# Moving the loop of spare blocks behind the static blocks in a mixture of experts, on one Trainium2 core

## The reference

```python
g_sel = argmax(softmax(h @ w_rg + b_rg))                  # 1 of 4 groups
e_p, e_idx = top_k(softmax(expert logits of that group), 2)  # 2 of its 8 experts
weights = g_p * e_p / sum(e_p)
# assignments sorted by expert, each expert's rows padded to blocks of 128
y = (silu(xb @ w_gate[e]) * (xb @ w_up[e])) @ w_down[e]   # one block of rows
out[token] += y * weight
```

## Time and profile before

| | us |
|---|---|
| median of 3 runs | 3689.51 (3687.7 to 3690.94) |
| the profiled execution | 3681.5 |
| its span, first to last instruction | 3679.7 |
| PE busy | 3420.4 (93%) |
| DVE busy | 1617.9 (44%) |
| ACT busy | 818.3 (22%) |
| POOL busy | 364.8 (10%) |

### The profile page before, as it was taken

How to read it: one execution, slowest core, us unless ns; L and a number is a source line. 1 busy time by engine, 2 the same in 40 slices (tenths; PEclk the granted TensorE clock), 3 DMA queues, 4 the chain that set the end, 5 groups by cost and what they waited for, 6 DMA issues and landing times. The chain is left out here.

```text
span 3679.7 us, 51768 instructions
## 1 busy us (share of the span) xinstructions
PE 3420.4 (93%) x20970; PEld 1738.1 (47%) x20970; DVE 1617.9 (44%) x2560; ACT 818.3 (22%) x1822; POOL 364.8 (10%) x355
## 2 busy tenths in 40 slices
PE   9999999899999899999998998998899978997996
PEld 4444665433333344777754333333455658553332
DVE  4750886510111475777756111113341875462114
ACT  0000650100000122555511000000233551111112
POOL 0010300210000000000000200000000820003110
PEclk9999999899999999999999999999999999999998
DMA  9990211599999621000023999997421402219996
GB/s 373 361 336 0 93 70 69 227 416 427 423 424 424 251 91 57 26 1 1 1 92 142 403 425 425 426 421 303 149 82 68 149 18 79 101 66 371 419 418 267
DMA packets 146694, 818.42 MB, mean 222 GB/s; under 512 B 29875, under 2 KB 35635, under 8 KB 100374
## 3 DMA queue, kind: packets, MB, share of 16 engines
q1 hardware_dynamic: 117910, 737.21, 50.1%
q0 software_dynamic: 25808, 68.88, 4.9%
q10 hardware_dynamic: 2736, 8.95, 0.6%
HBM read 752.52 MB, written 82.55 MB: 227 GB/s over the span
## 5 line engine op out<-in xcount | busy, mean ns | idle before, releaser
L2320 PE MATMUL m_yp<-m_w,m_hidT 128*32 128x512 f32 (+2 forms) x2248 | 378.9, 596 | 10.5 <-issue 4.6
L2297 PE MATMUL m_up<-m_w,m_xT 128*32 128x512 f32 (+2 forms) x1792 | 305.4, 608 | 20.3 <-DMA m_w<-in_moe_w_up 20.3
L2297 PE MATMUL m_gp<-m_w,m_xT 128*32 128x512 f32 (+2 forms) x1792 | 300.7, 598 | 9.8 <-DMA m_w<-in_moe_w_gate 5.4
L2078 DVE TENSOR_TENSOR m_hid<-m_sg,m_up 128x512 f32<-128x512 f32 x42 | 28.9, 688 | 573.9 <-PE m_up L2297 573.9
L2073 DVE TENSOR_TENSOR m_yt<-m_yp,keep_flat 128x512 f32<-128x512 f32 x128 | 82.5, 686 | 398.7 <-PE m_yp L2320 388.9
L2320 PEld LDWEIGHTS m_yp<-m_w,m_hidT 128*32 128x32 f32 (+2 forms) x2248 | 121.7, 124 | 219.6 <-issue 214.1
L2378 ACT ACTIVATE m_sg<-m_gp 128x512 f32<-128x512 f32 (+1 forms) x64 | 33.5, 524 | 786.1 <-PE m_gp L2297 539.2
L2297 PEld LDWEIGHTS m_up<-m_w,m_xT 128*32 128x32 f32 (+2 forms) x1792 | 104.2, 126 | 216.0 <-issue 216.0
L2297 PEld LDWEIGHTS m_gp<-m_w,m_xT 128*32 128x32 f32 (+2 forms) x1792 | 97.5, 124 | 206.7 <-issue 204.1
L434 PE MATMUL front_acc<-front_hT,front_wt 128*128 128x512 f32 x448 | 194.4, 594 | 0.4 <-DVE q0T L535 0.4
L1233 PE MATMUL n_acc<-n_wt,n_hT 128*128 128x512 f32 (+2 forms) x512 | 190.5, 528 | 2.0 <-DMA n_wt<-in_w_in 1.3
(11 more groups left out here) (505 smaller groups left out, 5032.8 us busy)
## 6 DMA issues: line engine op xcount, KB each, us to landing
m_w<-in_moe_w_gate SPq DMA_DIRECT2D x64, 2048.0 KB
m_w<-in_moe_w_up SPq DMA_DIRECT2D x64, 2048.0 KB
m_w<-in_moe_w_down SPq DMA_DIRECT2D x64, 2048.0 KB
v<-in_ada_w SPq DMA_DIRECT2D x40, 1024.0 KB
m_w<-in_moe_w_gate SPq DMA_DIRECT2D x32, 1024.0 KB
m_w<-in_moe_w_up SPq DMA_DIRECT2D x32, 1024.0 KB
m_w<-in_moe_w_down SPq DMA_DIRECT2D x32, 1024.0 KB, 30.2
v<-in_w_mod SPq DMA_DIRECT2D x24, 1024.0 KB
```

The lines of the kernel that those rows point to most:

```text
L2297: last = pe.matmul(acc[part, 0:F], xT[:, j, k, part], w[:, place_of[m_, r][0], k * F:(k + 1) * F], start=k == 0, stop=k == KC - 1)
L2320: last = pe.matmul(yp[e][part, :], hidT[:, k, part], w[:, place_of["d", r][0], k * D + e * 512:k * D + (e + 1) * 512], start=k == 0, stop= ...
```

## The change

Every engine's loop of spare blocks moves behind its static blocks. On SP all loads of the static blocks are issued without a stop, and the loads of the next stage's rows also come ahead of the loop; `AHEAD` goes, and a spare block now uses slots 0 to 2. On POOL the gather of block `DEEP` comes ahead of the spread and that of block `DEEP + 1` right behind it; the read of the table and its four operations become `sort_spills`, called in the loop over the static blocks at n = 3. Waits inside the loops' bodies are added, so that a spare block starts only when the static blocks are through; no body runs with these inputs. The computation of the static blocks is the same.

```diff
-    AHEAD = 2 * RING // 3
-    taken = {slot for _, _, slot, _ in layout.units[:AHEAD]}
-    spare = [s for s in range(RING) if s not in taken][:3]
+    spare = range(3)
...
                 place_rows()                       # DVE
-                for e in range(2):
-                    dve.sem_inc(so_y[e], 1)
-                spills = spilled(dve)
-                with dve.Fori(0, TURNS) as turn_no:
...
-                held(dve, st.marks, so_st, spills * (16 * GROUP) + 16)
                 copy_x(dve, dve.tensor_copy, 0, 0)
...
                 for e in range(2):
                     weigh_y(N - 1, e)
+                for e in range(2):
+                    dve.sem_inc(so_y[e], 1)
+                spills = spilled(dve)
+                with dve.Fori(0, TURNS) as turn_no:
...
-                for unit in layout.units[:AHEAD]:  # SP
+                for unit in layout.units:
                     load(*unit)
+                sp.wait_ge(d, at["gates"])
+                sp.wait_ge(sorted_out, 4)
+                for dst, row in ahead:
+                    sp.dma_start(dst, row).then_inc(ahead_in, 16)
+                sp.wait_ge(ahead_in, 16 * len(ahead))
                 spills = spilled(sp)
                 with sp.Fori(0, TURNS) as turn_no:
...
                 held(sp, st.marks, so_st, spills * (16 * GROUP) + 16)
-                for unit in layout.units[AHEAD:]:
-                    load(*unit)
...
+                def sort_spills():                 # POOL
+                    pool.wait_ge(t_st, 16 * 2 * T)
...
                 for n in range(DEEP):
                     gather(n)
+                gather(DEEP)
                 pool.wait_ge(filled, 16)
                 pool.wait_ge(d, at["places"])
                 for k in range(2):
                     for t in range(T):
                         pool.indirect_dma_start(out=row_table, ...).then_inc(t_st, 16)
-                pool.wait_ge(t_st, 16 * 2 * T)
...
+                gather(DEEP + 1)
+                for n in range(1, N):
+                    if n == 3:
+                        sort_spills()
+                    if n + DEEP + 1 < N:
+                        gather(n + DEEP + 1)
+                    scatter(n - 1)
+                scatter(N - 1)
                 spills = spilled(pool)
                 with pool.Fori(0, TURNS) as turn_no:
...
-                for n in range(DEEP, DEEP + 2):
-                    gather(n)
-                for n in range(1, N):
...
                 list_rows()                        # PE
+                keep_clock(pe, turn[0], ident, 4)
+                turn_x(0)
...
+                turn_hid(N - 1)
+                down(N - 1)
                 pe.sem_inc(so_dn, 1)
                 spills = spilled(pe)
                 with pe.Fori(0, TURNS) as turn_no:
...
                 act.sem_inc(so_st, 16)             # ACT
+                copy_x(act, act_copy, 0, 1)
...
+                copy_hid(N - 1)
                 spills = spilled(act)
                 with act.Fori(0, TURNS) as turn_no:
```

More of the change, by code:

```diff
@@ L2112, in _ @@
                     weigh_y(N - 1, e)
+                for e in range(2):
+                    dve.sem_inc(so_y[e], 1)
+                spills = spilled(dve)
+                with dve.Fori(0, TURNS) as turn_no:
+                    with dve.If(turn_no < spills):
+                        for j in range(GROUP):
+                            i = turn_no * GROUP + j
+                            dve.wait_ge(so_t, i + 1)
+                            dve.tensor_copy(xT[:, 0, half[0]], turn[0][:, :].rearrange("p (c s) -> p c s", c=4)).then_inc(so_cp[0], 1)
+                            dve.wait_ge(so_sg, i + 1)
+                            dve.tensor_tensor(hid[:, 0], sg[:, 0], up[0][:, 0:F], ALU.mult).then_inc(so_hid, 1)
+                            dve.wait_ge(stored[0], 16 * ((N + 1) // 2))
+                            dve.wait_ge(so_st, i * 16 + 16)
+                            dve.wait_ge(so_dn, i + 2)
+                            for e in range(2):
+                                dve.tensor_tensor(yt[:, 0, cols(e)], yp[e][:, :], gate[:, cols(e)], ALU.mult).then_inc(so_y[e], 1)
+                held(dve, st.marks, so_st, spills * (16 * GROUP) + 16)
             @block.sync
@@ L2135, in _ @@
                             expert = sp.value_load(ps[0:1, ds(i, 1)], min_val=0, max_val=LAYERS_EXPERTS - 1)
+                            sp.wait_ge(done["d"], N)
                             sp.wait_ge(so_dn, i + 1)
@@ L2166, in scatter @@
                                             bounds_check=2 * S - 1, oob_is_err=False).then_inc(stored[n % 2], 16)
+                def sort_spills():
+                    pool.wait_ge(t_st, 16 * 2 * T)
+                    with nc.allow_non_contiguous_dma(reason="one token number per row"):
+                        pool.dma_start(goal[:, LISTED:], row_table[LISTED * P:ROWS * P, :].rearrange("(b p) o -> p (b o)", p=P)).then_inc(spill_in, 16)
+                    pool.wait_ge(spill_in, 16)
+                    pool.tensor_copy(number_f, goal[:, LISTED:]).then_inc(sorted_out, 1)
+                    pool.wait_ge(sorted_out, 1)
+                    pool.tensor_scalar(second[:, LISTED:], number_f, float(S), -float(S), ALU.is_ge, ALU.mult).then_inc(sorted_out, 1)
+                    pool.wait_ge(sorted_out, 2)
+                    pool.tensor_tensor(number_f, number_f, second[:, LISTED:], ALU.add).then_inc(sorted_out, 1)
+                    pool.wait_ge(sorted_out, 3)
+                    pool.tensor_copy(ri[:, LISTED:], number_f).then_inc(sorted_out, 1)
+                    pool.wait_ge(sorted_out, 4)
                 pool.memset(empty[:, :], UNUSED_ROW).then_inc(e_set, 1)
@@ L2196, in _ @@
                             i = turn_no * GROUP + j
+                            for e in range(2):
+                                pool.wait_ge(stored[e], 16 * ((N + 1 - e) // 2))
                             pool.wait_ge(so_dn, i + 1)
@@ L2328, in _ @@
                 list_rows()
+                keep_clock(pe, turn[0], ident, 4)
+                turn_x(0)
+                gate_up(0)
+                turn_x(1)
+                for n in range(1, N):
+                    gate_up(n)
+                    turn_hid(n - 1)
+                    if n + 1 < N:
+                        turn_x(n + 1)
+                    down(n - 1)
+                turn_hid(N - 1)
+                down(N - 1)
                 pe.sem_inc(so_dn, 1)
@@ L2358, in _ @@
                             last.then_inc(so_dn, 1)
[L2359 to L2370, removed]
             @block.scalar
@@ L2396, in _ @@
                 act.sem_inc(so_st, 16)
+                copy_x(act, act_copy, 0, 1)
+                silu(0)
+                copy_x(act, act_copy, 1, 1)
+                for n in range(1, N):
+                    silu(n)
+                    copy_hid(n - 1)
+                    if n + 1 < N:
+                        copy_x(act, act_copy, n + 1, 1)
+                copy_hid(N - 1)
                 spills = spilled(act)
@@ L2408, in _ @@
                 held(act, st.marks, so_st, spills * (16 * GROUP) + 16)
[L2409 to L2417, removed]
 def tile_at(v, n):
```

15 lines of the change are left out of this document (removed).

## The result

The median of 14 runs is 3697.5 us (3687.5 to 3701.4), beside 3689.2 us (3686.1 to 3694.5) of the kernel before in the same runs. The ratio is 1.0018, with a 95% interval of 1.0011 to 1.0025: 6.6 us slower by the ratio (4.1 to 9.2); the bare medians lie 8.3 us apart. By the ratio the time is 3696 us, within the 0.2% and at the top of the range of 3679 to 3697, and the median itself lies 0.5 us above it. It is no zero, and the sum had +0.1 us. The profiled execution took 3692.9 us (span 3690.9), 11.4 us more than the one of before.

A forecast was written before the change was run, and what follows sets the result against it. Weight transfers at full DMA rate (about 425 GB/s) were taken to bound the mixtures, not PE. The profiled 3681.5 − 0.5 + 0.6 gave 3681.6 us; against the runs' median, 3689.5 + 0.1, rounded to 3689.6 us, range 3679 to 3697.

The forecast's parts named there:

- The rule: Mixture bodies: weight transfers never run dry, so PE's gain ahead of its last weight wait is waited away; 0 us.
- m0 against m1: First two mixtures before the change: PE started 5.2 us later in m1, yet last results came after 537.2 and 537.0 us.
- PE's start: First gate blocks: at most 5.9, 11.1 and 8.5 us earlier in the three mixtures; taken as 0 us of time.
- The third rival: Mixture start: first rows' gather may land late behind the weights, so PE's start doesn't move; 3689.6 us, chance 0.07.
- 17 us or more of waits for weights in m0: Sign of being right: in m0 PE's waits for weights grow by about as much as its first gate block comes earlier.
- SP's stop: SP's loads at mixture start: the pause between 6th and 7th load (12th and 13th in m2) goes; 0 us.
- the gathers ahead of the spread: POOL at mixture start: same bytes in another order, the spread's transfer cost stays; −0.5 us taken for m2.
- the read at n = 3: POOL amid static blocks: stands still 8.8 to 9.9 us, covered by rows gathered ahead; 0 us.
- The −0.5 us for m2: m2's spread: an earlier PE might heal a queue short of loads; 0 to −2.3 us, −0.5 taken.
- the loops at the end: Mixture end: loops hidden until SP reaches the barrier at 1232.5; bounds 0 and +3.8 us, +0.2 taken per mixture.
- signs of being wrong: First load to last result shrinks; PEldq, DVEq or POOLq reach the barrier behind SP; PE waits for rows after n = 3.
- the loops show at the end: Between last down and barrier: PE's long branch costs 3.8 us per mixture, DVE's slow loop 2.1; up to 3700.9, chance 0.14.

The follow-up runs named there:

- the delay experiment: Changed kernel with outer If(spills > 0) on all five engines, plus 30 or 60 more keep_clock matmuls before the first turn of x: 3709.5 and 3785.1 us, single runs.
- the second trace: Kernel before, and changed kernel, each profiled once more unchanged: mixture ends 7.7, 7.7, 8.0 us and 10.5, 10.2, 11.8 us behind the last result.

## Why the prediction was right, and where not

**The rule was right.** The bodies of the mixtures are set by the transfers. m0's last result came 537.2 us after the first load again, taking 1.6 to 8.1 us off the start brought nothing in either kernel, and the delay experiment gave the slack. m0 against m1 in the trace of before was a fair witness: 5.2 us are well inside 11 to 14 us. That the two agreed to 0.2 us was luck: in the second trace they stand at 537.7 and 539.7. For m2 I was unsure, because it waits for weights for only 1.9 us; it has 4 to 7 us of slack.

**PE's start** came 2.1, 8.1 and 7.2 us earlier, with bounds of 5.9, 11.1 and 8.5. DVE's plan, from which I took the bounds, was not what came last: it was the first gather (8.1 us of PE's wait in m0). The third rival had that mechanism, in part. I expected 17 us or more of waits for weights in m0, and there were 9.1 (12.4 before). In that trace the gain went elsewhere, into a first gate block at the lower clock and into the wait for ACT's copy, and in m0 nothing of it was left for the weights to take. That sign of being right did not come, though the last result did as forecast. In the second trace, where the third block did begin earlier, the waits for weights in m0 are 19.4 us.

**SP's stop, the gathers ahead of the spread, the read at n = 3**: 0 as taken. The −0.5 us for m2 didn't show, and is too small to show; with POOL's old order the time was the same (1.0017 against 1.0018).

**The step that failed is the one of the loops at the end**: "SP, which waits until it has landed, reaches the barrier at 1232.5. So other engines have until 1232.5 before they cost anything". That row is SP's first instruction behind the exit, not its arrival there. SP arrived at 1229.9 and was let go at 1232.4 by POOL's DRAIN. So there was a margin for every engine but one. One of the prediction's own signs of being wrong came true with it: POOL reached the exit behind SP (1229.8 against 1229.5 in m0). POOL's loop, for which I wrote that it "ends at 1232.2, just in time", is followed by the DRAIN, and of its 4.0 us in m0 2.8 are bare (the value is read while the scatter is still being issued). The terms are +2.8, +2.5 and +3.8 us, in place of +0.2 for each mixture: +9.1 in all, where the upper bound was 11.4. That the outcome is still "the same" is owed to the width of 0.2%, not to the sum. The runs' 6.6 us (4.1 to 9.2) agree at the edge of the interval; taking POOL's loop out again took off the whole difference, doubling it added 0.22% (8 us), and the traces say some 9 us for each of these.

The rival "the loops show at the end" was therefore the true case, with chance 0.14 and 0.08 for more than 7.4 us. It named the right place, but PE and DVE as the engines; that its price of 3.8 us, worked out from PE's long branch, is what m2 paid for POOL's loop is chance. Both lie hidden: PE's branch of 3562 ns cost nothing, and 5.3 us more on DVE cost nothing (exit 546.4 us behind the first load of m0, where the changed kernel had 541.1). Of the rule about jumps in the Trainium skill (Runtime: NRT & Kernel Launch, Instruction fetch mechanics): a long branch came back on PE in one mixture of three, again on the first jump over the body, and at the end it was off the path; the ends' times repeat to 0.1 us and hold no such stall. (The prediction calls this its third rival; in its list it is the second.) The long branch doesn't come at random either. It is in m1 in both traces of the kernel before (6.1 and 5.8 us) and in m0 in all seven traces in which PE turns its loop at the end (3.3 to 3.9 us), while in the other mixtures no such branch took over 0.5 us.

The 11.4 us between the two profiled executions are these 9.1 us and 2.7 us of later last results (0, 1.1, 1.6), the latter within what one kernel shows by itself, less 0.4 elsewhere. That last number is itself a sum of larger differences: the stretches between the mixtures came out 2.0 and 1.0 us shorter and the one behind m2 2.7 us longer.

## What to carry to other kernels

Before work is moved to the end of a block, look at the exit's own rows, one for each engine, and ask which DRAIN ends last. The first instruction behind a barrier only says when it opened, not who was late. Work on POOL, between its last DMA and the exit, cost here all of its length that lay behind the issue of that DMA (the second loop in full, the first less what ran beside the issue), while DVE could come 5 us later for nothing; a loop that is nearly always empty is best put behind one branch when it stands there. Where transfers set the body, a loop at the start was free, as long as it stayed inside the slack (here 4 to 14 us). And an engine that starts earlier only to wait has not gained: look at the second and third block too.

## What the runs showed of the hardware

- POOL's DRAIN at the exit of a mixture, where it has issued DMAs: 4878 to 4880 ns (5047 in m2) when it begins after the issue is over, whether that is 2.8 or 5.8 us before; when it begins earlier, it ends 4.9 us behind POOL's last instruction in m0 and m1, and 5.1 to 5.6 us in m2. In a block of the kernel before in which POOL only computed (L1482) it ended 0.1 us behind POOL's last instruction. The DRAINs of PE, DVE, ACT and SP with nothing left to do took 7 to 17 ns.
- POOL's queue ran ahead of its engine: the load of the loop's count began at 1225.8 us, before the scatter ahead of it started at 1226.04.
- A second empty loop of seven turns on POOL took 3.0 to 3.1 us. On PE a turn holds two branches of 221 ns, and in one mixture of three, always the same one for a kernel, the first jump over the body is longer (3562 ns here).
- Behind 8.1 us without work PE's granted clock was 0.50 of full speed (1.2 GHz) for the next 6 us, and a gate block took 9.40 us instead of 7.13.
